# The sparse layer of a two-block model: rotation sums on GpSimd instead of VectorE, and selection rounds ahead of the last value slot

## The chip, the cores and the metric

The kernel runs on one core of one Trainium2 chip. The metric is the time of one execution on the device in microseconds; the kernel before takes 1805.46 us (median of 3 runs, 1803.48 to 1808.78). Lower is better.

PE is TensorE (the matrix engine), PEld its weight loads, DVE is VectorE, ACT is ScalarE, POOL is GpSimd, SP is SyncE, whose queue issues DMAs.

## The reference, cut to what matters

The model is a hybrid layer (window attention, a recurrent mixer, gated linear attention) followed by a block with differential attention, a feed-forward layer, a sparse attention layer and a second feed-forward layer. Only the sparse layer is touched. With 528 tokens (16 meta tokens and 512 others; padding is left out by the kernel) it computes:

```python
q, k, v, qi, ki, wi = jnp.split(h @ w_in, DSA_SPLITS, axis=-1)
q = apply_rope(q.reshape(B, T, DSA_HEADS, DSA_HEAD_DIM), cos, sin) * (DSA_HEAD_DIM ** -0.5)
k = apply_rope(k.reshape(B, T, DSA_HEADS, DSA_HEAD_DIM), cos, sin)
qi = apply_rope(qi.reshape(B, T, IDX_HEADS, IDX_DIM), cos, sin)
ki = apply_rope(rms_norm(ki, idx_k_norm), cos, sin)
...
raw = jnp.einsum('bqhd,bkd->bqhk', qib, ki).astype(f32) * (IDX_DIM ** -0.5)
score = jnp.einsum('bqhk,bqh->bqk', jax.nn.relu(raw), wb.astype(f32))
...
top_val, top_idx = lax.top_k(score, topk)          # topk = 128
# attention of each query over its 128 selected keys only

def apply_rope(x, cos, sin):
    x1, x2 = jnp.split(x.astype(jnp.float32), 2, axis=-1)
    return jnp.concatenate([x1 * c - x2 * s, x2 * c + x1 * s], axis=-1)
```

## The kernel before, in words

**Projection of the sparse layer.** PE works through 29 groups, g0 to g28, each one weight slot: g0 is the index key, g1 to g4 the index queries, g5 to g12 the queries, g13 to g20 the keys, g21 to g28 the values. Each group is 8 k steps of 6 matmuls (two column halves, three products of high and low parts; L603 to L605). Three pairs of PSUM banks are used in turn, so group g may start only when DVE has read group g-3 (`dsa_free`, semaphores `rope_read` and `v_ch`).

**Weights.** POOL issues for each group a load of the slot that was freed (`high_load`, L1004, waits for `slot_used`), ACT writes its negative (L1049), and POOL issues an accumulating load onto that (`low_sum`, L1011, waits for `w_negated`). Four slots are in flight.

**Rotations.** `rope(i, ...)` on DVE takes two groups each. i is 8 and 9 for the index queries (400 columns), 10 to 13 for the queries and 14 to 17 for the keys (528 columns). Four products read PSUM and the tables (L1358 to L1361; the last signals `rope_read`), and then the difference and the sum of products in SBUF follow (L1363, L1364; the last signals `rope_done`). On `rope_done` SP issues eight DMAs that place the heads (`dsa_scatter`, L1815, signals `scattered`). The first index score of PE, inside g7 behind its second k step, waits until both index-query scatters (8 and 9) have landed.

**Index scores and selection.** For each of four tiles of queries (n = 1, 4, 2, 3) four units of two score matmuls (L945) are placed between the k steps of g7 to g12; ACT takes the relu (L1271), DVE adds the weighted result (`index_sums`, L1665 and L1667). ACT may reuse a relu buffer only when DVE has added the unit two before. Then DVE finds the 128 best keys: 14 rounds per tile (`take_eight`: MAX8 at L1678, match and replace at L1679), and one instruction at the end of a tile makes a mask (L1682). 56 rounds in all. The table `ROUNDS_AT` says how many rounds stand behind the work of each group; those that are left stand between the value slots (`rounds_between`). DVE executes in program order.

**Behind the projection.** DVE scales each value group (L1714), PE turns it (L639) and ACT copies it (L1103, L1104). Then `dsa_attention` runs: scores on PE (L656), minimum and bias on DVE (L1502, needs the masks), exponentials on ACT (L1181), normalising on DVE (L1512), transposes on PE (L669), values on PE (L689). DVE's first L1502 stands in program order behind every selection round.

Of the kernel before, what the change touches and what calls it, by code (L numbers as in the profile page):

```python
# [18 lines left out]
T2 = T1 + META  # L19
# [43 lines left out]
S_DSA = S_DOWN0 + N_DOWN  # L63
# [6 lines left out]
def build(nc, ins, out_t):  # L70
# [3 lines left out]
    ALU = mybir.AluOpType  # L74
# [8 lines left out]
    def sem(name):  # L83
        return ctx.enter_context(nc.semaphore(name))
# [245 lines left out]
    LATER = slice(P, T2)  # L330
# [20 lines left out]
    def rope_t(i, j):  # L351
        return rope_buf[:, i % 2, j, :]
# [29 lines left out]
    S = {n: sem(n) for n in names}  # L382
# [9 lines left out]
    def halves(v):  # L392
        return v.rearrange("p (a b) -> p a b", a=2)
# [100 lines left out]
        return min((n + 1) * P, T2)  # L494

    G_QI, G_Q, G_K, G_V = 1, 5, 13, 21
    ROUNDS_AT = {8: 3, 10: 4, 12: 3, 13: 2, 14: 3, 15: 2, 16: 3, 17: 2, 18: 2, 19: 2, 20: 2}
    IDX_UNITS = [(n, p) for n in (1, 4, 2, 3) for p in range(4)]
    IDX_AT = {7: (0, 4), 8: (4, 8), 9: (8, 10), 10: (10, 12), 11: (12, 14), 12: (14, 16)}

# [60 lines left out]
    def w_turn(n):  # L561
        return (n - S_DA) % W_RING, 16 * ((n - S_DA) // W_RING + 1)

    def split_at(n):
        r = w_turn(n)[0]
        return w_hi[:, r, :], w_lo[:, r, :]
# [428 lines left out]
    def pool_block2(pool):  # L995
        g = nc.gpsimd

        def high_load(n):

            if n >= N_SLOTS:  # L1000
                return
            if n >= S_DA + W_RING:
                pool.wait_ge(S["slot_used"], n - W_RING + 1)
            g.dma_start(split_at(n)[0], ins["weights"][n]).then_inc(hi_loaded[w_turn(n)[0]], 16)  # L1004

        def low_sum(n):

            if n >= N_SLOTS:
                return
            pool.wait_ge(S["w_negated"], n - S_DA + 1)  # L1010
            g.dma_start(split_at(n)[1], ins["weights"][n], accum_op=ALU.add).then_inc(lo_summed[w_turn(n)[0]], 16)  # L1011

        def output_rests(base):

            for k in range(KT):
                pool.wait_ge(S["o_hi"], base + k + 1)
                g.tensor_tensor(o_lo[:, k, :], oT[:, k, :], o_hi[:, k, :].bitcast(F32), ALU.subtract).then_inc(S["o_split"], 1)

        pool.wait_ge(S["hn_ready"], 3 * KT)
        for n in range(S_DA, S_DA + W_RING):  # L1020
            high_load(n)
        for n in range(S_DA, S_DA + W_RING - 1):
            low_sum(n)
        pool.wait_ge(S["norm_var"], 3)
        g.memset(da_qlast, 0.0).then_inc(S["zeroed"], 1)
        for n in range(S_DA, N_SLOTS):
            if n == S_DSA + 6:
                pool.wait_ge(S["norm_var"], 5)
                g.memset(qlast, 0.0).then_inc(S["zeroed"], 1)
            if n == S_DSAO:  # L1030
                output_rests(8)
            high_load(n + W_RING)
            low_sum(n + W_RING - 1)


    def weight_high(act, n):
# [266 lines left out]
    def vector_block2(ve, st):  # L1303
        V = nc.vector
# [39 lines left out]
        def rope(i, s0, g):  # L1344

            ve.wait_ge(S["slot_used"], s0 + g + 2)
            if i >= 2:
                ve.wait_ge(scattered[i % 2], 128 * (i // 2))
            if i in (8, 9):
                a, b = (psum[:, 2 * (x % 3), 0:NL] for x in (g, g + 1))  # L1350
                c, s = cosT[:, LATER], sinT[:, LATER]
                x0, x1, x2, x3 = whole = [rope_t(i, j)[:, LATER] for j in range(4)]
            else:
                a, b = pair(g), pair(g + 1)
                c, s = cos2, sin2
                whole = [rope_t(i, j) for j in range(4)]
                x0, x1, x2, x3 = (halves(x) for x in whole)
            V.tensor_tensor(x0, a, c, ALU.mult)  # L1358
            V.tensor_tensor(x1, b, s, ALU.mult)
            V.tensor_tensor(x2, a, s, ALU.mult)  # L1360
            V.tensor_tensor(x3, b, c, ALU.mult).then_inc(S["rope_read"], 1)  # L1361
            ve.wait_ge(S["rope_read"], i + 1)
            V.tensor_tensor(whole[0], whole[0], whole[1], ALU.subtract)  # L1363
            V.tensor_tensor(whole[3], whole[3], whole[2], ALU.add).then_inc(S["rope_done"], 1)  # L1364

        def values(s0, g0, base):

# [320 lines left out]
        taken = 0  # L1688
        for g in range(7, G_V + 1):
            if g % 2:  # L1690
                i = 10 + (g - 7) // 2
                rope(i, S_DSA, g - 2)
                if i == 16:
                    ve.wait_ge(S["zeroed"], 3)
                    for c in range(2):
                        r = slice(64 * c, 64 * c + 64)
                        last = V.tensor_copy(qlast[r, :, 16 * c:16 * c + 16], qs[r, :, 4 * P:T2])
                    last.then_inc(S["q_last"], 1)
            for u in range(*IDX_AT.get(g, (0, 0))):
                index_sums(u)  # L1700
            for r in range(taken, taken + ROUNDS_AT.get(g, 0)):
                take_eight(r)
            taken += ROUNDS_AT.get(g, 0)
        left = 4 * ROUNDS - taken

        def rounds_between(j):

            for r in range(taken + left * j // 8, taken + left * (j + 1) // 8):
                take_eight(r)
        for j in range(8):  # L1710
            ve.wait_ge(S["slot_used"], S_DSA + G_V + j + 1)
            if j >= 2:
                ve.wait_ge(S["v_tr"], 8 + j - 1)
            V.tensor_tensor(halves(vch[:, j % 2, :]), pair(G_V + j), rs2, ALU.mult).then_inc(S["v_ch"], 1)  # L1714
            rounds_between(j)
        dsa_attention()
        residual(5, S_DSAO, 1, 16, lambda k: col("ffn_norm", 8 + k))
        ffn(1, 5, S_UP1, S_DOWN1, 24)
# [1308 lines left out]
```

## Time and profile before

| | |
|---|---|
| median of 3 runs | 1805.46 us |
| the profiled execution | 1798.56 us |
| its span, first to last instruction | 1796.8 us |
| mean granted clock of TensorE | 0.975 |
| PE busy | 1713.8 us (95%) |
| DVE busy | 949.0 us (53%) |
| ACT busy | 632.5 us (35%) |
| POOL busy | 330.8 us (18%) |

The span is what the trace covers; the profiled execution has 1.8 us around it. Busy times of a span say which engine is full on average. For a change in one stage what counts is which engine ends last there, and that is read from gaps in PE's timeline and from what ended them.

### The profile page before, as it was taken

Reading aid. Unit: us, or ns where it says so; the run is one execution under the profiler, and the core shown is the slowest. Engines: PE = TensorE matmul, PEld = TensorE weight load, DVE = VectorE, ACT = ScalarE, POOL = GpSimd, SP = SyncE. Lnnn points to the kernel's source line nnn. Section 1 sums busy time; section 2 is a strip of 40 time slices with the busy share of each in tenths; the row PEclk is TensorE's granted clock in tenths of the full one; section 3 lists DMA queues with packets and bytes.
Section 4 is the critical chain, followed back from the end, with each engine's and each line's share of the span. In section 5 each row is a group of like instructions: output and inputs, shape, how many; then the busy total and the mean of one; then the engine's idle time right before and its main releaser. Section 6 shows DMA issues by size and latency. Waiting matters only on the chain.

```text
span 1796.8 us, 33090 instructions
## 1 busy us (share of the span) xinstructions
PE 1713.8 (95%) x14293; PEld 1537.7 (86%) x14293; DVE 949.0 (53%) x1881; ACT 632.5 (35%) x1095; POOL 330.8 (18%) x450
## 2 busy tenths in 40 slices
PE   7999989979998899999999999999899999999997
PEld 3777679859996589999999998799669999999886
DVE  5237695435335865655562115787883555565003
ACT  3354442243114653222222222322584322222222
POOL 0001102001220012222222222122012222222221
PEclk9999969899998999999999999999999999999999
DMA  7521400126994039898888999699305888898995
GB/s 301 177 76 59 176 1 4 61 53 145 226 207 93 1 69 195 181 180 184 180 184 185 199 194 203 145 212 210 79 2 111 175 184 186 181 185 182 197 209 139
DMA packets 81794, 266.46 MB, mean 148 GB/s; under 512 B 11648, under 2 KB 15360, under 8 KB 81520
## 3 DMA queue, kind: packets, MB, share of 16 engines
q0 software_dynamic: 59040, 214.98, 56.7%
q1 hardware_dynamic: 18592, 43.57, 7.0%
q10 hardware_dynamic: 4016, 5.78, 1.1%
q8 instruction: 113, 1.85, 0.4%
q14 instruction: 33, 0.27, 0.0%
HBM read 252.49 MB, written 2.10 MB: 142 GB/s over the span
## 4 chain that ended last, share of the span: by engine, by line
PE 76%; DVE 7%; issue 2%; DMA 1%; ACT 1%; POOL 0%; ACTq 0%; DVEq 0%; POOLq 0%
PE banks L603 21%; PE banks L604 20%; PE banks L605 20%; PE banks L2090 3%; PE banks L656 1%; PE banks L669 1%; DMA w_lo<-in_weights 1%; DVE stat L1407 1%; PE banks L689 1%; PE banks L1845 1%; PE banks L1847 1%; PE banks L1846 1%; PE banks L732 1%; PE banks L945 1%; DVE arena L1417 1%
## 5 line engine op out<-in xcount | busy, mean ns | idle before, releaser
L603 PE MATMUL banks<-hn_hi,w_hi 128*128 128x264 f32 (+2 forms) x2216 | 637.9, 288 | 14.4 <-DMA w_lo<-in_weights 12.8
L604 PE MATMUL banks<-hn_lo,w_hi 128*128 128x264 f32 (+2 forms) x2216 | 631.4, 285 | 0.0
L605 PE MATMUL banks<-hn_hi,w_lo 128*128 128x264 f32 (+2 forms) x2216 | 630.8, 285 | 0.0
L1049 ACT ACTIVATE w_lo<-w_hi 128x1024 fp32r<-128x1024 f32 x205 | 217.2, 1060 | 771.9 <-DMA w_hi<-in_weights 757.3
L603 PEld LDWEIGHTS banks<-hn_hi,w_hi 128*128 128x128 f32 x2216 | 419.0, 189 | 26.8 <-issue 22.3
L604 PEld LDWEIGHTS banks<-hn_lo,w_hi 128*128 128x128 f32 x2216 | 420.2, 190 | 0.7 <-issue 0.2
L605 PEld LDWEIGHTS banks<-hn_hi,w_lo 128*128 128x128 f32 x2216 | 417.9, 189 | 0.3
L1004 POOL DMA_DIRECT2D w_hi<-in_weights x205 | 114.1, 557 | 915.3 <-PE banks L605 840.3
L1011 POOL DMA_DIRECT2D w_lo<-in_weights x205 | 180.8, 882 | 156.1 <-ACT w_lo L1049 146.8
L603 PE MATMUL banks<-a_hi,w_hi 128*128 128x264 f32 (+1 forms) x506 | 160.4, 317 | 1.6 <-DVE u_in L1576 0.8
L604 PE MATMUL banks<-a_lo,w_hi 128*128 128x264 f32 (+1 forms) x506 | 160.8, 318 | 0.0
L605 PE MATMUL banks<-a_hi,w_lo 128*128 128x264 f32 (+1 forms) x506 | 160.7, 318 | 0.0
L603 PEld LDWEIGHTS banks<-a_hi,w_hi 128*128 128x128 f32 x506 | 95.3, 188 | 8.5 <-DVE u_in L1576 1.0
L605 PEld LDWEIGHTS banks<-a_hi,w_lo 128*128 128x128 f32 x506 | 95.2, 188 | 6.6
L604 PEld LDWEIGHTS banks<-a_lo,w_hi 128*128 128x128 f32 x506 | 95.0, 188 | 6.8
L1301 DVE TENSOR_TENSOR ring_r<-ring,ring_r 128x1024 fp32r<-128x1024 f32 x32 | 39.6, 1236 | 80.5 <-ACT ring_r L1043 80.4
L1578 DVE TENSOR_TENSOR u_in<-banks,rs 128x516 f32<-128x516 f32 x44 | 30.6, 695 | 90.5 <-PE banks L605 90.4
L1576 DVE TENSOR_TENSOR u_in<-banks,rs 128x528 f32<-128x528 f32 x44 | 31.1, 707 | 88.5 <-PE banks L605 88.4
L1846 PE MATMUL banks<-h_r,ring_r 128*128 128x512 f32 x192 | 76.0, 396 | 0.0
L603 PE MATMUL banks<-o_hi,w_hi 128*128 128x264 f32 (+1 forms) x256 | 73.3, 286 | 1.4 <-DMA w_lo<-in_weights 0.8
L604 PE MATMUL banks<-o_lo,w_hi 128*128 128x264 f32 (+1 forms) x256 | 72.6, 284 | 0.0
L605 PE MATMUL banks<-o_hi,w_lo 128*128 128x264 f32 (+1 forms) x256 | 72.4, 283 | 0.0
(426 smaller groups left out, 2702.5 us busy)
## 6 DMA issues: line engine op xcount, KB each, us to landing
w_hi<-in_weights POOLq DMA_DIRECT2D x205, 512.0 KB, 5.2
w_lo<-in_weights POOLq DMA_DIRECT2D x205, 512.0 KB, 7.2
ring<-in_weights SPq DMA_DIRECT2D x49, 512.0 KB, 4.5
arena<-arena ACTq DMA_DIRECT2D x64, 66.0 KB, 5.3
arena<-arena SPq DMA_DIRECT2D x64, 66.0 KB, 4.9
arena<-in_gate_w SPq DMA_DIRECT2D x8, 512.0 KB, 3.5
h<-in_xT SPq DMA_DIRECT2D x2, 1024.0 KB, 6.3
arena<-in_alibi SPq DMA_DIRECT2D x1, 1024.0 KB, 7.7
```

Of the source, the lines that this page charges most:

```text
L603: mm(o, w[0][:, j, :], x[0][:, k, lo:hi], start=first, stop=False)
L604: mm(o, w[0][:, j, :], x[1][:, k, lo:hi], start=False, stop=False)
L605: ins_ = mm(o, w[1][:, j, :], x[0][:, k, lo:hi], start=False, stop=last)
L656: last = mm(psum[:, 2 * (v % 2) + c, 0:keys(n)], qs[r, p, n * P:(n + 1) * P], kz[r, p, 0:keys(n)], start=True, stop=True)
L1004: g.dma_start(split_at(n)[0], ins["weights"][n]).then_inc(hi_loaded[w_turn(n)[0]], 16)
L1011: g.dma_start(split_at(n)[1], ins["weights"][n], accum_op=ALU.add).then_inc(lo_summed[w_turn(n)[0]], 16)
L1049: nc.scalar.activation(split_at(n)[1], split_at(n)[0].bitcast(F32), ACT.Copy, scale=-1.0).then_inc(S["w_negated"], 1)
L1301: nc.vector.tensor_tensor(ring_lo(n), ring_slot(n), ring_hi(n).bitcast(F32), ALU.subtract).then_inc(S["w_split_d"], 1)
L1576: V.tensor_tensor(halves(u_in[:, g % 4, 2:T2 + 2]), pair(g), rs2, ALU.mult).then_inc(S["u_evac"], 1)
L1578: V.tensor_tensor(halves(u_in[:, g % 4, KEEP + 2:T2 + 2]), kept_pair(g), halves(rs[:, KEEP:T2]), ALU.mult).then_inc(S["u_evac"], 1)
L1846: mm(out, w[0][:, k, :], x_lo, start=False, stop=False)
L2090: last = mm(out(s), lhs[r], rhs[r], start=start, stop=stop)
```

## The change

Ten rotations of the sparse layer (i = 8 to 17) lose their last two instructions on DVE. POOL executes them in a new function `rope_sums`, placed behind the `high_load` and the `low_sum` of iterations 3, 5, ..., 21 of the sparse layer's groups: iteration 3 for i = 8, iteration 5 for i = 9, and so on. SP's scatters still wait for `rope_done`, which POOL now signals.

The table of rounds changes, and the rounds that are left (28 before, 20 now) are spread over seven value slots instead of eight, so that none stands behind the last.

```diff
-    ROUNDS_AT = {8: 3, 10: 4, 12: 3, 13: 2, 14: 3, 15: 2, 16: 3, 17: 2, 18: 2, 19: 2, 20: 2}
+    ROUNDS_AT = {8: 4, 10: 5, 12: 5, 13: 2, 14: 4, 15: 2, 16: 3, 17: 2, 18: 4, 19: 2, 20: 3}
+    SUMS_AT = tuple(range(3, 23, 2))
...
+        def rope_sums(i):
+
+            t = LATER if i < 10 else slice(0, T2)
+            x0, x1, x2, x3 = (rope_t(i, j)[:, t] for j in range(4))
+            pool.wait_ge(S["rope_read"], i + 1)
+            g.tensor_tensor(x0, x0, x1, ALU.subtract)
+            g.tensor_tensor(x3, x3, x2, ALU.add).then_inc(S["rope_done"], 1)
...
             high_load(n + W_RING)
             low_sum(n + W_RING - 1)
+            if n - S_DSA in SUMS_AT:
+                rope_sums(SUMS_AT.index(n - S_DSA) + 8)
...
             V.tensor_tensor(x3, b, c, ALU.mult).then_inc(S["rope_read"], 1)
+            if i >= 8:
+                return
             ve.wait_ge(S["rope_read"], i + 1)
-            V.tensor_tensor(whole[0], whole[0], whole[1], ALU.subtract)
-            V.tensor_tensor(whole[3], whole[3], whole[2], ALU.add).then_inc(S["rope_done"], 1)
+            V.tensor_tensor(rope_t(i, 0), rope_t(i, 0), rope_t(i, 1), ALU.subtract)
+            V.tensor_tensor(rope_t(i, 3), rope_t(i, 3), rope_t(i, 2), ALU.add).then_inc(S["rope_done"], 1)
...
-            for r in range(taken + left * j // 8, taken + left * (j + 1) // 8):
+            for r in range(taken + left * j // 7, taken + left * (j + 1) // 7):
                 take_eight(r)
...
-            rounds_between(j)
+            if j < 7:
+                rounds_between(j)
```

**POOL, around the sums of rotation 9.** These are POOL's instructions behind g4 and g5, before; w_hi is the load of a slot, w_lo the accumulating one, and the memset prepares a buffer of the attention.

```order
L1004 DMA w_hi<-in_weights 128x1024 [waits slot_used]
L1011 DMA w_lo<-in_weights 128x1024 [waits w_negated]
L1004 DMA w_hi<-in_weights 128x1024 [waits slot_used]
L1011 DMA w_lo<-in_weights 128x1024 [waits w_negated]
L1029 MEMSET arena 128x256 [waits norm_var]
```

The same place now:

```order
L1005 DMA w_hi<-in_weights 128x1024 [waits slot_used]
L1012 DMA w_lo<-in_weights 128x1024 [waits w_negated]
L1005 DMA w_hi<-in_weights 128x1024 [waits slot_used]
L1012 DMA w_lo<-in_weights 128x1024 [waits w_negated]
L1025 TENSOR_TENSOR arena<-arena 128x400 [waits rope_read]
L1026 TENSOR_TENSOR arena<-arena 128x400
L1038 MEMSET arena 128x256 [waits norm_var]
```

The sums of rotation 9 stand behind a load that waits for the end of g5, on an engine that had no such work there.

**DVE, between the index sums in g12 and rotation 13.** Before, three rounds of the first tile stand there, then the four products and the two sums:

```order
L1671 TENSOR_TENSOR arena<-arena,causalf 128x128 [waits i_acc]
L1672 MEMSET arena 128x16
L1678 MAX top<-arena 128x8 [waits dve_step]
L1679 MATCH_REPLACE arena<-top,arena 128x240 [waits dve_step]
L1678 MAX top<-arena 128x8 [waits dve_step]
L1679 MATCH_REPLACE arena<-top,arena 128x240 [waits dve_step]
L1678 MAX top<-arena 128x8 [waits dve_step]
L1679 MATCH_REPLACE arena<-top,arena 128x240 [waits dve_step]
L1358 TENSOR_TENSOR arena<-banks,arena 128x528 [waits scattered1,slot_used,dve_step]
```

Now there are five, with the mask instruction of the tile behind them (of the five, the last three):

```order
L1690 MAX top<-arena 128x8 [waits dve_step]
L1691 MATCH_REPLACE arena<-top,arena 128x240 [waits dve_step]
L1690 MAX top<-arena 128x8 [waits dve_step]
L1691 MATCH_REPLACE arena<-top,arena 128x240 [waits dve_step]
L1690 MAX top<-arena 128x8 [waits dve_step]
L1691 MATCH_REPLACE arena<-top,arena 128x240 [waits dve_step]
L1694 TENSOR_SCALAR arena<-arena 128x256 [waits dve_step]
L1368 TENSOR_TENSOR arena<-banks,arena 128x528 [waits scattered1,slot_used,dve_step]
L1369 TENSOR_TENSOR arena<-banks,arena 128x528
L1370 TENSOR_TENSOR arena<-banks,arena 128x528
L1371 TENSOR_TENSOR arena<-banks,arena 128x528
```

Two rounds and the mask instruction moved ahead of the first product of rotation 13.

**DVE, behind the last value slot.** Before, four rounds (here the last two) and the mask stand between the scaling of the last slot and the first score unit of the attention:

```order
L1678 MAX top<-arena 128x8 [waits dve_step]
L1679 MATCH_REPLACE arena<-top,arena 128x496 [waits dve_step]
L1678 MAX top<-arena 128x8 [waits dve_step]
L1679 MATCH_REPLACE arena<-top,arena 128x496 [waits dve_step]
L1682 TENSOR_SCALAR arena<-arena 128x512 [waits dve_step]
L1502 ISA arena,stat<-banks,causalf 128x128 [waits a_sc,sel_spread,dve_step]
```

Now:

```order
L1690 MAX top<-arena 128x8 [waits dve_step]
L1691 MATCH_REPLACE arena<-top,arena 128x496 [waits dve_step]
L1694 TENSOR_SCALAR arena<-arena 128x512 [waits dve_step]
L1726 TENSOR_TENSOR arena<-banks,rs 128x528 [waits v_tr,slot_used,dve_step]
L1514 ISA arena,stat<-banks,causalf 128x128 [waits a_sc,sel_spread]
```

The last scaling stands directly ahead of the attention's first instruction.

## Rows read from the trace of the kernel before

**Rows 1.** Windows: length, busy PE, PEld, DVE, ACT, POOL, clock, DMA, GB/s.

```profile
1123.00:1181.00 58.00, 56.50 (x389) 44.34 (x388) 41.97 (x91) 21.16 (x39) 10.35 (x15) 1.00 0.68 155
1181.00:1228.00 47.00, 46.66 (x386) 46.69 (x387) 41.31 (x85) 8.32 (x8) 11.37 (x16) 1.00 0.99 224
```

**Rows 2.** Timeline, PE: start, us, line, tile, count, [idle before and its releaser].

```profile
1124.22 0.68 PE L945 MATMUL banks<-arena 64*128 64x240 f32 x4 [1.11 <-issue]
1181.35 0.36 PE L603 MATMUL banks<-hn_hi,w_hi 128*128 128x264 f32 x1 [0.71 <-DVE arena L1361]
...
1274.03 0.93 PE L656 MATMUL banks<-arena 64*128 64x128 f32 x8
1279.56 3.36 PE L656 MATMUL banks<-arena 64*128 64x384 f32 x8 [4.60 <-DVE stat L1502]
```

**Rows 3.** Timeline, DVE, from the last value slot to the attention.

```profile
1271.98 0.71 DVE L1714 TENSOR_TENSOR arena<-banks,rs 128x528 f32<-128x528 f32 x1 [1.12 <-issue]
...
1278.53 0.43 DVE L1682 TENSOR_SCALAR arena<-arena 128x512 f32<-128x512 f32 x1
1278.99 0.29 DVE L1502 CUSTOM_DVE_ANT_0 arena<-banks,causalf 128x128 f32<-128x128 f32 x1
...
1282.22 0.16 DVE L1509 RECIPROCAL stat<-stat 128x2 f32<-128x2 f32 x1
```

**Rows 4.** Timeline, ACT, the first exponentials of the attention.

```profile
1274.89 1.28 ACT L1181 ACT_TABLE_LOAD   x1
1279.33 0.40 ACT L1181 ACTIVATE arena<-arena,stat 128x128 f32<-128x128 f32 x1 [3.15 <-DVE stat L1502]
```

**Rows 5.** Timeline, SP: the first and last of rotation 9's eight scatters.

```profile
1113.30 0.51 SPq L1815 DMA_DIRECT2D arena<-arena  x1
1117.66 0.59 SPq L1815 DMA_DIRECT2D arena<-arena  x1
```

**Rows 6.** Line L1815: landing of all 80, then of the one at 1117.66.

```profile
DMA to landing us min/median/max: 2.0/4.7/7.3
DMA to landing us min/median/max: 6.5/6.5/6.5
```

**Rows 7.** Timeline, POOL, behind g5.

```profile
1116.17 0.55 POOL L1004 DMA_DIRECT2D w_hi<-in_weights  x1 [4.36 <-PE banks L605]
1116.71 0.91 POOL L1011 DMA_DIRECT2D w_lo<-in_weights  x1
1117.25 0.69 POOL L1029 MEMSET arena<- 128x256 f32 x1
```

**Rows 8.** Lines by shape, POOL: busy us, mean ns; idle before.

```profile
L1017 POOL TENSOR_TENSOR o_lo<-arena,o_hi 128x528 fp32r<-128x528 f32 x8 | 10.4, 1310 | 77.3 <-ACT o_hi L1199 77.3
L2254 POOL TENSOR_TENSOR arena<-norm_tmp 128x256 f32<-128x256 f32 x7 | 6.4, 910 | 0.0
```

**Rows 9.** Windows behind two gaps of PE: clock is the third from last.

```profile
429.00:433.00 4.00, 3.99 (x20) 3.99 (x21) 1.17 (x4) 1.06 (x1) 0.87 (x1) 0.57 1.06 236
1279.50:1282.80 3.30, 3.24 (x8) 1.19 (x8) 2.20 (x12) 2.63 (x11) 0.00 (x0) 0.50 0.00 0
```

**Rows 10.** Timeline, PE, the gap ahead of the first of these windows.

```profile
429.01 0.39 PE L603 MATMUL banks<-hn_hi,w_hi 128*128 128x264 f32 x1 [2.39 <-DMA w_lo<-in_weights]
```

**Rows 11.** Timeline, DVE: index sums, rounds, products of rotation 11.

```profile
1142.88 1.51 DVE L1667 SCALAR_TENSOR_TENSOR arena<-arena,wtok 16x512 f32<-16x512 f32 x2 [1.11 <-ACT arena L1271]
...
1144.64 0.41 DVE L1678 MAX8 top<-arena 128x8 f32<-128x240 f32 x1
...
1147.50 0.71 DVE L1358 TENSOR_TENSOR arena<-banks,arena 128x528 f32<-128x528 f32 x1
...
1149.35 0.69 DVE L1361 TENSOR_TENSOR arena<-banks,arena 128x528 f32<-128x528 f32 x1
...
1157.27 1.24 DVE L1667 SCALAR_TENSOR_TENSOR arena<-arena,wtok 128x368 f32<-128x368 f32 x2 [2.28 <-ACT arena L1271]
...
1173.91 1.50 DVE L1667 SCALAR_TENSOR_TENSOR arena<-arena,wtok 128x496 f32<-128x496 f32 x2 [2.63 <-ACT arena L1271]
```

More of the change, by code:

```diff
@@ L1351, in rope @@
                 c, s = cosT[:, LATER], sinT[:, LATER]
-                x0, x1, x2, x3 = whole = [rope_t(i, j)[:, LATER] for j in range(4)]
+                x0, x1, x2, x3 = (rope_t(i, j)[:, LATER] for j in range(4))
             else:
@@ L1355, in rope @@
                 c, s = cos2, sin2
-                whole = [rope_t(i, j) for j in range(4)]
-                x0, x1, x2, x3 = (halves(x) for x in whole)
+                x0, x1, x2, x3 = (halves(rope_t(i, j)) for j in range(4))
             V.tensor_tensor(x0, a, c, ALU.mult)
```

## The prediction

> **What bounds the kernel now.** I read the window view first, then the gaps in PE's timeline, then what stands around each gap on the other engines. In the projection of the sparse layer PE is the engine that ends last: from 1123 to 1181 us it is busy 56.5 of 58 us at the full clock while DVE has 42 and POOL 10 [rows 1]. So work taken off DVE is worth nothing there by itself. What counts are the few gaps of PE, and there are four that the change touches [rows 2]: 1.11 us ahead of the first index score in g7, no gap but little margin at g10, 0.71 us at the start of g14 behind the products of rotation 13, and 4.60 us ahead of the attention's third score unit, which waits for DVE. Each is priced below. One more thing is to be seen in the windows: behind a gap of some us PE may run at the lower of its two levels, 1.2 instead of 2.4 GHz.
>
> Times are those of the profiled execution, which lasts 1798.56 us with a span of 1796.8; the median of the runs is 6.9 us above. I work out a difference and add it to the median.
>
> **Part 1, no rounds behind the last value slot.** DVE scales the last value group at 1271.98, ends four rounds at 1278.53 (some 1.48 us each) and a mask of 0.43, and starts the first score unit at 1278.99 [rows 3]. PE has the first two score units done in the 0.93 us from 1274.03 [rows 2], so the first of them is there at about 1274.5, and DVE could start at 1274.6: 4.4 us earlier. Who is late next? ACT: its table load is a row from 1274.89 for 1.28 us, so its first exponential can start at 1276.2 and not before, against 1279.33 now [rows 4]: 3.1 us earlier. But PE gains as well. Its third and fourth score units took 3.36 us at the lower level [rows 2, 9], because a gap of 4.60 stood ahead of them; with a gap of about half a microsecond I take them at full clock, 1.7 us. DVE's third unit then ends near 1277.0, the first exponentials near 1277.1, and normalising starts at 1277.1 where it started at 1282.22 [rows 3]: 5.1 earlier. ACT, 3.1 earlier at first, has the table load behind it after that and only follows DVE; I take it that it makes up the rest within the first units. So -5.0 us. Bounds: -3.1 if ACT stays the late one, and -6.1 if the 4.4 and the whole 1.7 of clock came through. The rounds that moved ahead between the value slots cost nothing: three rounds and the scaling are 5.2 us, and a value group is longer on PE, as the 1.12 us of idle ahead of the last scaling, behind three rounds of this size, shows [rows 3].
>
> **Part 2, the sums of rotation 9 and the first index score.** Now SP's scatters of rotation 9 are issued from 1113.30, the last at 1117.66 [rows 5]; that last one lands 6.5 us after its issue [rows 6], at 1124.1, and PE's first index score starts at 1124.22 after waiting 1.11 [rows 2]. The trace calls the releaser "issue"; the two times agree to 0.1 us, so I take it for this landing. In the changed order the sums stand on POOL behind the load that waits for the end of g5 (1116.17) and the accumulating load (1116.71). The memset that stands at that place starts at 1117.25 [rows 7], and so can the sums. No row shows a sum of 400 columns on POOL: 528 columns take 1.31 us, 256 take 0.91 [rows 8], so between 0.91 and 1.31, and by interpolation 1.1; two end at 1119.4. That is 6.1 us later than SP's start now. The eight issues take 4.4 to the last (1113.30 to 1117.66), so the last is issued at 1123.8. Its landing is the unknown: all 80 lie between 2.0 and 7.3 us [rows 6]. A scatter issued right behind a pair of weight loads was the slow one (6.5, with the pair at 1116.17 and 1116.71), and the next pair is issued within half a microsecond of 1123.8, so I take 5.4. The landing is at 1129.2, with bounds 1125.8 and 1131.1; PE starts again at 1129.3 where it started at 1124.22. That is +5.1 us, bounds +1.7 and +7.0. PE cannot use the wait, since its instructions are executed in order and the scores stand in front of the rest of g7. What it costs beyond the wait is the clock. The gap is 6.2 us. Behind a gap of 2.39 the window of 4 us ran at a mean of 0.57, which is about 3.4 us at half level [rows 9, 10], and behind 4.60 there were 3.3 us at 0.50 [rows 9]. Behind 1.11 and 0.71 nothing was lost. Half of 3.4 is +1.7 us; bounds 0 and +2.1. Part 2 together: +6.8.
>
> Rotation 8's sums wait on POOL for their products, which DVE finishes late, so that scatter moves by 1 us only and stays ahead of rotation 9's. The other eight scatters also start later, but what waits for them is the rotation two further, four groups away. POOL's weight loads move by nothing: a pair of sums of 528 columns is 2.6 us and POOL idles 4.36 us ahead of such a load [rows 7].
>
> **Part 3, more rounds where DVE has no room.** In g7 to g12 DVE's index sums are tied to PE through ACT: the idle of 1.11, 2.28 and 2.63 us ahead of them [rows 11] is where the 1.3 us that each rotation saves on DVE vanish. Behind the last index sum of a group nothing is saved, and what is added there is late in full. A round of the first tile costs 0.95 us (three from 1144.64 to 1147.50). At g8 one is added: the last product of rotation 11 ends at 1150.04 now [rows 11] and would end 0.95 later, against PE's own course. PE shows no gap at g10 now, so it gets there at 1150.1 or later, and how much later no row tells: between 0 and +0.95, and I take the middle, +0.5. At g10 one is added ahead of rotation 12's products; PE shows no gap at g12, and DVE idles 2.28 inside g10 [rows 11]: 0 (to +0.95). At g12 two are added and the tile's mask, 0.3 us (one of 512 columns takes 0.43 [rows 3]): 2 x 0.95 + 0.3 = 2.2. PE already waits 0.71 for exactly these products at g14 [rows 2], so all of it is on the path: +2.2 (1.9 to 2.4), and the gap becomes 2.9. Between g13 and g15 six rounds of 1.5 us and the four products of 2.5 give 11.4, against two groups of PE. A group has 48 matmuls, and a window of 47 us without scores holds 386 of them [rows 1], 5.84 a group, 11.7 for two: no wait, though with little to spare. From there on DVE does no more between two rotations than that.
>
> **A rule that speaks against the change.** The idle that covers DVE's index sums is between 1.11 and 2.63 us [rows 11], and the sums of rotations 10 to 12 on POOL would lie beside them. The Trainium skill (GPSIMD Engine Reference, Key points) states that GpSimd shares its SBUF interfaces with VectorE and that the two contend where a DVE instruction has two SBUF inputs, as the index sums have. No row of before shows the two side by side in this stage. By that rule a rotation could hold DVE for up to POOL's 2.6 us, of which 2.28 is covered at rotation 11: 0.3 us more in the sum, which I leave out.
>
> **The sum.** -5.0 + 5.1 + 1.7 + 0.5 + 2.2 = +4.5 us: 1805.46 + 4.5 = 1810.0. A difference of 0.3% or 5.4 us is about what a measurement of this kernel can tell from none, so this is "within 0.3%", on the slow side.
>
> **Rivals.**
> 1. Two clock drops: slower by over 0.3%. The gap at g14 grows to 2.9 us, and a gap of 2.39 was enough once [rows 9, 10]. If the level falls there too, another 1.7 is paid. It decides from a gap of somewhere between 1.11 and 2.39. Against it: that gap stood in another stage, with the DMA queues late. With it +4.5 + 1.7 = +6.2, and with the landing at its late bound +8.1: about 1812.6. Chance 0.43, including a landing near the late bound without the second drop.
> 2. The landing is early: the last scatter lands in 2.0 us and the level stays. Part 2 is +1.7, the sum -5.0 + 1.7 + 0.5 + 2.2 = -0.6: 1804.9. For it speaks the low end of the 80 landings, against it the weight loads issued at the same time. Chance 0.12, within 0.3%.
> 3. What ended PE's wait at 1124.1 was not the landing, so the later sums cost nothing: -5.0 - 0.4 + 0 to 2.2, some -3 to -6: about 1801. For it: the releaser is not named. Against: the agreement to 0.1 us, and that the code has PE wait for this. Chance 0.07, which I count as faster.
> 4. The forecast itself: 0.38.
>
> Faster by over 0.3%: 0.07; within: 0.50 (the forecast and rival 2); slower: 0.43. The sum of all low bounds is 1.7 + 0 + 0 + 1.9 - 6.1 = -2.5, of all high bounds 7.0 + 2.1 + 0.95 + 0.95 + 2.4 + 1.7 - 3.1 = +12. Both ends at once are unlikely; I give -1 to +10.5, that is 1804.5 to 1816.
>
> **What would show it.** PE's gap ahead of the first index score: 6 us instead of 1.1, with SP's scatters of rotation 9 issued from about 1119.4, and the clock at half for some 3 us behind it. The gap at g14: 2.9 instead of 0.7, released by the fourth product of rotation 13. A gap of under 0.5 us at g10. The gap of 4.60 ahead of the attention's third unit gone, and the full clock there. The eight 528-column sums of POOL near 1.3 us. The prediction is wrong if the gap in g7 stays near 1 us, if the attention starts less than 3 us earlier against the end of g28, or if DVE's index sums grow beside POOL's.

## The result and the profile after

The changed kernel takes 1808.7 us (median of 17 runs, 1803.5 to 1814.9), beside 1801.4 us for the kernel before (17 runs, 1794.0 to 1808.8). The ratio is 1.0044, with a 95% interval of 1.0031 to 1.0057: by it the change is 7.9 us slower (5.6 to 10.3); the two medians by themselves are 7.3 us apart. The forecast was +4.5, 1810.0 us; the sign and the mechanism were right, and rival 1, with a second clock drop, is nearer in size.

One execution of each has a trace. The one of before took 1798.56 us, the one of the change 1804.37, a difference of 5.8; but the part ahead of the stage was 2.8 us shorter in the second. So I measure the stage between two marks on PE, one ahead of and one behind everything that was changed: the fold matmul ahead of the index queries' end, and the first group of four transposes in the attention. PE's timeline, before and then the change:

```profile
1103.43 1.13 PE L929 MATMUL banks<-arena,fold 128*128 128x512 f32 x2 [0.91 <-DVE arena L1646]
...
1285.06 0.66 PE L669 MATMUL banks<-ident,arena 128*128 128x128 f32 x4 [1.25 <-DVE arena L1512]
```

```profile
1100.59 0.70 PE L930 MATMUL banks<-arena,fold 128*128 128x512 f32 x1 [1.55 <-DVE arena L1658]
...
1127.62 1.17 PE L946 MATMUL banks<-arena 64*128 64x240 f32 x4 [7.37 <-issue]
...
1156.63 0.36 PE L604 MATMUL banks<-hn_hi,w_hi 128*128 128x264 f32 x1 [0.97 <-DVE arena L1371]
...
1190.05 0.36 PE L604 MATMUL banks<-hn_hi,w_hi 128*128 128x264 f32 x1 [2.96 <-DVE arena L1371]
...
1285.49 1.82 PE L657 MATMUL banks<-arena 64*128 64x384 f32 x8 [0.29 <-DVE stat L1514]
...
1290.09 0.66 PE L670 MATMUL banks<-ident,arena 128*128 128x128 f32 x4 [1.09 <-DVE arena L1524]
```

The stage took 1285.06 - 1103.43 = 181.6 us and now takes 1290.09 - 1100.59 = 189.5: 7.9 us longer, the same as by the ratio. Three of the gaps of [rows 2] are there again, larger or smaller (1.11, 0.71 and 4.60 are now 7.37, 2.96 and 0.29), and there is one at g10 that had been none. Between the marks the 7.9 divide so:

| stretch | before | after | more | of it |
|---|---|---|---|---|
| fold to first index score | 20.79 | 27.03 | +6.2 | gap 1.11 to 7.37 |
| to the start of g14 | 57.13 | 62.43 | +5.3 | g10 0.97, g14 2.25, the rest (2.1) clock |
| to DVE's last scaling | 90.63 | 92.18 | +1.6 | clock |
| to the first normalising | 10.24 | 5.18 | -5.1 | no rounds, clock at full |
| to the second mark | 2.84 | 2.68 | -0.2 | |

The clock is the third number from the last in these windows of the change; they stand inside g7's gap, behind it, behind the gap at g14, and at the attention's start:

```profile
1124.00:1127.60 3.60, 0.00 (x0) 0.01 (x1) 0.00 (x0) 0.00 (x0) 0.00 (x0) 0.71 0.88 184
1127.60:1132.20 4.60, 4.58 (x18) 3.73 (x20) 0.81 (x2) 0.63 (x2) 0.00 (x0) 0.50 0.02 4
1190.00:1194.00 4.00, 3.96 (x20) 3.99 (x21) 3.83 (x9) 1.06 (x1) 2.57 (x2) 0.57 0.97 226
1284.00:1290.00 6.00, 3.88 (x26) 1.68 (x23) 4.67 (x23) 5.59 (x17) 0.00 (x0) 1.00 0.72 168
```

Behind the first gap 4.6 us ran at 1.2 GHz, behind the second 4.0 us at a mean of 0.57. That is 2.3 and 1.7 us of PE's time, close to the 2.1 and 1.6 left over in the table. The attention, which ran at 0.50 before [rows 9], runs at 1.00. In the last 3.6 us of PE's wait in g7 every engine stands: DVE, ACT and POOL have 0.00.

Why it stands is read on POOL and SP. POOL behind g5, in the change (answers to [rows 7]):

```profile
1113.32 0.55 POOL L1005 DMA_DIRECT2D w_hi<-in_weights  x1 [4.31 <-PE banks L606]
...
1114.42 1.42 POOL L1025 TENSOR_TENSOR arena<-arena 128x400 f32<-128x400 f32 x1
1115.43 1.41 POOL L1026 TENSOR_TENSOR arena<-arena 128x400 f32<-128x400 f32 x1
```

SP's first and last scatter of rotation 9, and, from the view of that line, the landing of the last:

```profile
1116.87 0.51 SPq L1828 DMA_DIRECT2D arena<-arena  x1
...
1121.22 0.59 SPq L1828 DMA_DIRECT2D arena<-arena  x1
```

```profile
DMA to landing us min/median/max: 6.3/6.3/6.3
```

The sums stand behind the load that waits for PE's end of g5, and end at 1116.84. SP issues from 1116.87, the last at 1121.22; it lands 6.3 us later, at 1127.5, and PE starts at 1127.62. Counted from the fold, SP starts at 16.3 instead of 9.9, 6.4 later.

DVE at the end of the projection, answering to [rows 3], and ACT, answering to [rows 4]:

```profile
1282.23 0.71 DVE L1726 TENSOR_TENSOR arena<-banks,rs 128x528 f32<-128x528 f32 x1 [0.86 <-PE banks L606]
...
1284.92 0.29 DVE L1514 CUSTOM_DVE_ANT_0 arena<-banks,causalf 128x128 f32<-128x128 f32 x1 [1.99 <-PE banks L657]
...
1287.41 0.16 DVE L1521 RECIPROCAL stat<-stat 128x2 f32<-128x2 f32 x1
```

```profile
1285.14 1.28 ACT L1192 ACT_TABLE_LOAD   x1
1286.44 0.40 ACT L1192 ACTIVATE arena<-arena,stat 128x128 f32<-128x128 f32 x1
```

The rows between scaling and score units are gone; DVE now waits 1.99 us for PE.

What I had left out of the sum is on DVE beside POOL's sums. These are the index sums behind rotation 11's products, first before and then in the change; the last two index sums behind rotation 12's; and the mask of a later tile beside the sums of a later rotation. Behind them stand POOL's sums of rotation 11:

```profile
1151.84 3.15 DVE L1667 SCALAR_TENSOR_TENSOR arena<-arena,wtok 128x368 f32<-128x368 f32 x5
```

```profile
1156.84 6.12 DVE L1679 SCALAR_TENSOR_TENSOR arena<-arena,wtok 128x368 f32<-128x368 f32 x5
1163.69 1.24 DVE L1679 SCALAR_TENSOR_TENSOR arena<-arena,wtok 128x368 f32<-128x368 f32 x2 [0.74 <-ACT arena L1282]
...
1180.37 1.51 DVE L1679 SCALAR_TENSOR_TENSOR arena<-arena,wtok 128x496 f32<-128x496 f32 x2 [0.17 <-ACT arena L1282]
...
1216.26 3.55 DVE L1694 TENSOR_SCALAR arena<-arena 16x528 f32<-16x528 f32 x1
```

```profile
1157.06 1.67 POOL L1025 TENSOR_TENSOR arena<-arena 128x528 f32<-128x528 f32 x1
1158.36 1.64 POOL L1026 TENSOR_TENSOR arena<-arena 128x528 f32<-128x528 f32 x1
```

Five index sums take 6.12 us where they took 3.15: the 3.0 us lost on DVE are the length of POOL's pair, 2.94 us from 1157.06 to 1160.00. The idle that covered DVE's index sums, 2.28 at this place [rows 11], is down to 0.74, and one group later 2.63 is down to 0.17. It is not used up, so PE does not see it; but at rotation 12 little is left.

Each of these POOL sums is recorded with 1.6 to 1.7 us where 1.31 was known [rows 8]. That is not DVE's doing. The two sums of 400 columns above took 1.42 and 1.41 while DVE stood idle (it has no instruction between 1109.3 and 1118.85). In the change the long ones are those directly behind a load that POOL has just issued; those of rotations 8 and 13, for which POOL waited on DVE first, took 1.05 and 1.31. In both cases the second sum starts as soon behind the first (1.01 and 1.3 us); it is the end of the last one that comes some 0.4 us later. Why was not tried.

### The profile page after: what moved, and what is told of

Same layout as the page of the kernel before. It is cut to its first block, busy times and chain, and to the rows that moved or that the text cites. A ratio compares the mean times of both kernels' runs of the same rounds, so it can differ in the third digit from the quotient of the medians.

```text
span 1802.5 us, 33090 instructions
## 1 busy us (share of the span) xinstructions
PE 1714.8 (95%) x14293; PEld 1540.8 (85%) x14293; DVE 948.9 (53%) x1861; ACT 632.5 (35%) x1095; POOL 356.2 (20%) x470
## 4 chain that ended last, share of the span: by engine, by line
PE 76%; DVE 7%; issue 2%; DMA 1%; ACT 1%; POOL 0%; ACTq 0%; DVEq 0%
PE banks L604 20%; PE banks L605 20%; PE banks L606 20%; PE banks L2103 3%; DMA w_lo<-in_weights 1%; PE banks L670 1%; PE banks L657 1%; DVE stat L1419 1%; PE banks L690 1%; PE banks L1858 1%; PE banks L1859 1%; PE banks L1860 1%; PE banks L946 1%; PE banks L733 1%; DVE arena L1429 1%
```

## The experiments

My theory: the wait in g7 and the clock behind it are the loss, and they come from where the sums of rotations 8 and 9 stand on POOL, not from how long they take. The rivals: contention between POOL and DVE makes DVE late; or the rounds in their new places do. Each ratio is against the kernel before, run beside it; "us" is that ratio times the median of the kernel before. "Stage" is the time between the two marks in the one trace, against 181.6 before.

| | ratio (95%) | us | stage |
|---|---|---|---|
| the change | 1.0044 (1.0031 to 1.0057) | +7.9 | +7.9 |
| e1 rounds only | 0.9996 (0.9976 to 1.0017) | -0.7 | -0.1 |
| e2 sums only | 1.0022 (1.0006 to 1.0038) | +4.0 | +8.6 |
| e3 change, 8 and 9 back on DVE | 0.9970 (0.9953 to 0.9987) | -5.4 | -0.9 |
| e4 change, 9 one place earlier | 0.9987 (0.9970 to 1.0004) | -2.3 | +4.6 |
| e5 before, with idle sums on POOL | 1.0027 (1.0010 to 1.0044) | +4.9 | +5.9 |
| e6 rounds fitted, sums on DVE | 0.9952 (0.9939 to 0.9966) | -8.7 | -6.7 |
| e7 the same, 13 to 17 on POOL | 0.9961 (0.9941 to 0.9980) | -7.0 | -5.5 |
| e8 only 8 and 9 on POOL | 1.0043 (1.0026 to 1.0060) | +7.8 | +8.8 |
| e9 change with fitted rounds | 1.0001 (0.9983 to 1.0019) | +0.2 | +2.8 |
| e10 e6 with two queues | 0.9963 (0.9940 to 0.9985) | -6.7 | -5.8 |

The stage column is on average 2.3 us above the other. One trace of before is behind all of it, so its stage may simply have been a short one; a term of under 2 us is therefore read from gaps and not from a median. Some of it is the clock: the traces of e4, e8, e9 and e10 lost 1.7 to 3.4 us at the very start of the stage, where the edits change nothing or next to nothing, and the one of before did not. The column also leaves out what comes behind the second mark. There the traces of e1, e6 and e10 fell to 1.2 GHz, at a cost of 1.7 us each; this is e1:

```profile
1286.00:1289.00 3.00, 3.00 (x16) 1.76 (x14) 2.22 (x9) 1.61 (x8) 0.00 (x0) 0.50 0.00 0
```

The traces of the change, e3, e4, e7 and e9 have the same short gaps of PE ahead of that place (0.84 and 1.09 us) and lost nothing. So the full clock in the attention is not a sure part of what the end gives back.

**e1 and e2: the two halves.** e1 is the kernel before with the new table and seven slots; e2 is the change with the old ones.

```diff
-    ROUNDS_AT = {8: 3, 10: 4, 12: 3, 13: 2, 14: 3, 15: 2, 16: 3, 17: 2, 18: 2, 19: 2, 20: 2}
+    ROUNDS_AT = {8: 4, 10: 5, 12: 5, 13: 2, 14: 4, 15: 2, 16: 3, 17: 2, 18: 4, 19: 2, 20: 3}
...
-            for r in range(taken + left * j // 8, taken + left * (j + 1) // 8):
+            for r in range(taken + left * j // 7, taken + left * (j + 1) // 7):
                 take_eight(r)
...
-            rounds_between(j)
+            if j < 7:
+                rounds_between(j)
```

> The table of rounds and the seven slots of the change, with all sums back on VectorE. Theory (the waits of TensorE price the change): no long gap ahead of the first index score (1.1 us as before), the attention starts 5.0 us earlier against the last value slot; g10 waits 0.9, g14 waits 2.9 with one clock drop (1.7), and g16 waits about 1.0, since six rounds, two sums and four products are 12.7 us against 11.7 of TensorE. Sum -5.0 + 0.9 + 2.2 + 1.7 + 1.0 = +0.8 us against before. Rival (GpSimd and VectorE contend for the SBUF interface, and that is what the change costs): without GpSimd's sums the 5 us of the end come through, -5 us.

PE's timeline of e1:

```profile
1124.69 0.68 PE L945 MATMUL banks<-arena 64*128 64x240 f32 x4 [1.46 <-issue]
...
1151.60 0.36 PE L603 MATMUL banks<-hn_hi,w_hi 128*128 128x264 f32 x1 [0.96 <-DVE arena L1361]
...
1185.00 0.36 PE L603 MATMUL banks<-hn_hi,w_hi 128*128 128x264 f32 x1 [2.95 <-DVE arena L1361]
...
1197.77 0.36 PE L603 MATMUL banks<-hn_hi,w_hi 128*128 128x264 f32 x1 [0.92 <-DVE arena L1361]
```

The gaps at g10 and g14 are those of the change to 0.01 us, with no sum on POOL: they belong to the rounds alone. At g16 there is one of 0.92 that the change does not have; there the saved sums are what hides a round. The three gaps cost about what the end gives back, and 0.9996 says the same, within some 4 us either way. One thing differs: behind this gap of 2.95 us no clock was lost.

```profile
1185.00:1189.00 4.00, 4.00 (x33) 4.00 (x34) 3.90 (x8) 1.06 (x1) 0.00 (x0) 1.00 1.02 242
```

The same edit the other way round, in the change (e2):

```diff
-    ROUNDS_AT = {8: 4, 10: 5, 12: 5, 13: 2, 14: 4, 15: 2, 16: 3, 17: 2, 18: 4, 19: 2, 20: 3}
+    ROUNDS_AT = {8: 3, 10: 4, 12: 3, 13: 2, 14: 3, 15: 2, 16: 3, 17: 2, 18: 2, 19: 2, 20: 2}
```

> The ten pairs of sums on GpSimd as in the change, with the old table and the old eight slots. Theory: the gap ahead of the first index score is 7.4 us as in the change, with the clock at half behind it; g14 waits 0.7 as before, g10 nothing; the gap of 4.6 us ahead of the attention's third unit stays. Sum +6.3 + 1.7 = +8.0 us against before. Rival (contention): VectorE's index sums grow by 3 us per rotation and what they delay makes up part of it: gaps at g10 or g14 larger than before.

PE's timeline of e2:

```profile
1131.03 1.17 PE L946 MATMUL banks<-arena 64*128 64x240 f32 x4 [7.38 <-issue]
...
1288.66 1.65 PE L657 MATMUL banks<-arena 64*128 64x384 f32 x4 [4.60 <-DVE stat L1514]
```

The wait in g7 is there in full, and the others are as before (0.72 at g14, 4.60 in the attention). Its trace has +8.6, its median only +4.0 (1.1 to 6.9): slower, but by less than expected, and that stays open.

**e8: rotations 8 and 9 alone on POOL**, the old rounds, all else on DVE. In the change:

```diff
-    SUMS_AT = tuple(range(3, 23, 2))
+    SUMS_AT = (3, 5)
...
-            g.tensor_tensor(x3, x3, x2, ALU.add).then_inc(S["rope_done"], 1)
+            g.tensor_tensor(x3, x3, x2, ALU.add).then_inc(S["pool_done"], 1)
...
-            if i >= 8:
+            if i in (8, 9):
                 return
```

(SP waits for `pool_done` for these two, and the table and the slots are those of before.)

> Only the sums of rotations 8 and 9 on GpSimd, at the places of the change; those of 10 to 17 on VectorE, old table, old eight slots. Theory (the change's cost is the first index score): the gap ahead of it is 7.4 us, with one clock drop, the others as before: +6.3 + 1.7 = +8 us. Rival (the run with all ten on GpSimd measured only +4, so the drop or part of the wait is often absent): +4 us, with a shorter gap. If contention had been in that run's time, this one is faster than it.

PE's timeline, and the window behind the gap:

```profile
1131.06 1.17 PE L946 MATMUL banks<-arena 64*128 64x240 f32 x4 [6.16 <-issue]
```

```profile
1131.00:1136.50 5.50, 5.44 (x22) 4.04 (x23) 0.81 (x2) 0.81 (x3) 0.00 (x0) 0.51 0.50 121
```

1.0043: these four instructions, moved from DVE to POOL, make by themselves a loss as large as the whole change. Without the other eight rotations on POOL it is not faster than e2, so contention is not what e2 pays for. The gap is 1.2 us shorter than in e2, because the last scatter landed 5.1 us behind its issue and not 6.3. Of the 8.8 in the trace 1.7 is not the edit's: behind a gap of 1.25 us ahead of the first mark this window ran at a mean of 0.72 (0.28 of 6.0).

```profile
1104.00:1110.00 6.00, 5.81 (x25) 5.21 (x25) 2.56 (x9) 1.06 (x1) 2.27 (x3) 0.72 0.83 189
```

**e3: those two back on DVE**, with their two instructions each behind the products again, and the change otherwise:

```diff
-    SUMS_AT = tuple(range(3, 23, 2))
+    SUMS_AT = tuple(range(7, 23, 2))
...
-            if i >= 8:
+            if i >= 10:
                 return
```

> The change with the sums of rotations 8 and 9 back on VectorE; GpSimd keeps those of 10 to 17. Theory: the gap ahead of the first index score is 1.1 us again, the rest as in the change: -5.0 + 1.0 + 2.25 + 1.7 = -0.1 us against before, some 8 us faster than the change. Rival (contention): the index sums still grow by 3 us beside GpSimd, and the kernel stays clearly slower than before, +4 us or more.

PE's timeline of e3, then DVE's, and the window behind the gap at g14:

```profile
1123.48 0.68 PE L946 MATMUL banks<-arena 64*128 64x240 f32 x4 [1.77 <-issue]
...
1150.39 0.36 PE L604 MATMUL banks<-hn_hi,w_hi 128*128 128x264 f32 x1 [0.96 <-DVE arena L1371]
...
1183.78 0.36 PE L604 MATMUL banks<-hn_hi,w_hi 128*128 128x264 f32 x1 [2.96 <-DVE arena L1371]
```

```profile
1150.60 6.12 DVE L1681 SCALAR_TENSOR_TENSOR arena<-arena,wtok 128x368 f32<-128x368 f32 x5
```

```profile
1183.80:1187.80 4.00, 4.00 (x33) 4.00 (x34) 3.83 (x9) 1.06 (x1) 2.53 (x2) 1.00 0.96 210
```

The long wait is gone, and what remains is faster than before (0.9970). The index sums still take 6.12 us and the gap at g10 is still the 0.96 of e1, which has no sum on POOL: contention is real and costs nothing here. The gap of 2.96 again lost no clock. I had expected -0.1, with a second clock drop of 1.7 in it that this trace does not have. The median is 4.5 us below what the trace's stage gives; beyond the 2.3 that holds for the column, this is open.

**e4: the sums of rotation 9 one place earlier**, behind the loads that wait for g4:

```diff
-    SUMS_AT = tuple(range(3, 23, 2))
+    SUMS_AT = (3, 4) + tuple(range(7, 23, 2))
```

> The change with GpSimd's sums of rotation 9 one iteration ahead, behind the loads that follow g4 instead of g5. Theory (the place in GpSimd's queue sets the wait): the sums start when their products are there, SP starts about 1.2 us later than before the change instead of 6.4, and the gap ahead of the first index score is 2 to 3 us instead of 7.4; one clock drop may go with it. Sum -5.0 + 1.5 + 1.0 + 2.25 + 1.7 = +1.5, with a drop in g7 +3.2 us against before. Rival (GpSimd's slower arithmetic or its DMA work makes the sums late wherever they stand): the gap stays above 5 us.

POOL's timeline at the sums of rotation 9, and PE's at the first index score:

```profile
1115.81 1.05 POOL L1025 TENSOR_TENSOR arena<-arena 128x400 f32<-128x400 f32 x1 [0.40 <-DVE arena L1371]
1116.82 1.05 POOL L1026 TENSOR_TENSOR arena<-arena 128x400 f32<-128x400 f32 x1
```

```profile
1128.61 1.17 PE L946 MATMUL banks<-arena 64*128 64x240 f32 x4 [1.95 <-issue]
```

On POOL the sums now wait for DVE's product and not for a load, and PE's gap is 1.95 us, not 7.37. The sums are still there, recorded 0.4 us shorter each now that POOL idles just ahead of them: it is their place in POOL's queue that cost. Its trace lost clock from 1104 on (3.4 us of PE's time), behind the 1.95 us in g7 (1.7) and behind a gap of 2.95 at g14 (1.7; a mean of 0.57 over 4 us). The median has less of it: by the ratios e4 is 10.2 us faster than the change (-2.3 against +7.9).

**e5: contention by itself.** The kernel before, with eight pairs of two-input operations of 528 columns on POOL where the change has the sums of rotations 10 to 17. They work on an unused tile and nothing reads what they write.

```diff
+            if n - S_DSA in range(7, 23, 2):
+                ...
+                for a in range(2):
+                    g.tensor_tensor(sq[:, a, :], sq[:, 0, :], sq[:, 1, :], ALU.subtract).then_inc(S["idle_sum"], 1)
```

> The kernel before, and on GpSimd eight extra pairs of 528-column two-input operations on a buffer nobody uses, at the places where the change has the sums of rotations 10 to 17; VectorE keeps all its work and all rounds stand where they did. It prices the contention alone. Theory (contention is real and hidden): VectorE's five index additions of 368 columns take 6.1 us instead of 3.15, those of 496 columns 7.2 instead of 3.8, the gaps of TensorE stay 1.1, 0.7 and 4.6 us but for some tenths at g14, and the time is that of before within 0.1% (-1 to +2 us). Rival (contention costs time): +4 us or more, with new gaps at g10 to g16. If the additions keep their length, there is no contention.

PE's timeline, and DVE's at rotation 13:

```profile
1182.86 0.36 PE L603 MATMUL banks<-hn_hi,w_hi 128*128 128x264 f32 x1 [1.18 <-DVE arena L1369]
...
1234.51 0.36 PE L603 MATMUL banks<-hn_hi,w_hi 128*128 128x264 f32 x1 [1.48 <-DVE arena L1369]
```

```profile
1182.75 2.61 DVE L1371 TENSOR_TENSOR arena<-arena 128x528 f32<-128x528 f32 x1
1185.28 1.83 DVE L1372 TENSOR_TENSOR arena<-arena 128x528 f32<-128x528 f32 x1
```

My expectation fell. PE waits at five rotations (0.47 more, 0.63, 1.29, 0.87, 1.48, together 4.7 us), and the median is +4.9. DVE's own sums of 0.7 us each took 2.61 and 1.83 beside POOL's. So two inputs from SBUF on both engines cost PE time as soon as DVE is near its limit. In the change they do not, because there DVE has given its sums away and has products from PSUM and rounds at these places, which keep their length (one mask does not, at 1216.26 above, and PE shows no gap behind it). The Trainium skill (GPSIMD Engine Reference, Key points) states that the two engines contend where DVE's instruction has two SBUF inputs; the rows agree, and the page gives no size for it.

**e6: rounds placed without POOL.** Since e1's gaps are products that come too late, I counted rounds to DVE's room at each place and left the sums on DVE:

```diff
-    ROUNDS_AT = {8: 3, 10: 4, 12: 3, 13: 2, 14: 3, 15: 2, 16: 3, 17: 2, 18: 2, 19: 2, 20: 2}
+    ROUNDS_AT = {8: 3, 10: 4, 12: 2, 13: 3, 14: 3, 15: 2, 16: 3, 17: 2, 18: 3, 19: 2, 20: 3}
...
-            for r in range(taken + left * j // 8, taken + left * (j + 1) // 8):
+            first = taken + sum((4, 4, 4, 4, 4, 3, 3)[:j])
+            for r in range(first, first + (4, 4, 4, 4, 4, 3, 3)[j]):
                 take_eight(r)
...
-            rounds_between(j)
+            if j < 7:
+                rounds_between(j)
```

> All sums on VectorE, none of the change's GpSimd work; rounds placed by room: 3 at g8, 4 at g10, 2 at g12, then 3, 3, 2, 3, 2, 3, 2, 3, and 4, 4, 4, 4, 4, 3, 3 between the value slots, none behind the last. Theory: the gap at g14 (0.7) goes, no gap at g10 and g16, the attention starts 5.0 us earlier: -5.7 us or 0.9968 of before. Rival (VectorE has no room for the rounds without GpSimd's help): new gaps of more than 1 us in the key groups or the value slots, and less than 3 us gained.

PE's timeline, and two windows:

```profile
1121.70 0.68 PE L945 MATMUL banks<-arena 64*128 64x240 f32 x4 [0.67 <-issue]
...
1271.72 1.82 PE L656 MATMUL banks<-arena 64*128 64x384 f32 x8 [0.29 <-DVE stat L1502]
```

```profile
1116.00:1180.00 64.00, 63.32 (x448) 51.26 (x447) 44.81 (x95) 22.24 (x40) 11.73 (x16) 1.00 0.71 159
1180.00:1268.00 88.00, 88.00 (x733) 87.89 (x733) 80.65 (x175) 20.16 (x27) 20.01 (x28) 1.00 0.96 212
```

0.9952 (0.9939 to 0.9966), faster than both kernels: the end's 5 us are taken, and from 1180 on PE is busy 88.00 of 88 us, with no gap at g10, g14 or g16. Nothing had to go to POOL for it. I had expected -5.7; of the -6.7 in the trace 5.1 is the end, 0.7 the gap at g14 and 0.4 the smaller gap in g7. The -8.7 by the median is more than these give, and that is open.

**e7 and e9: what POOL adds to that.** e7 is e6 with the sums of rotations 13 to 17 on POOL, e9 is the change (all ten on POOL) with e6's rounds.

```diff
-    SUMS_AT = tuple(range(3, 23, 2))
+    SUMS_AT = tuple(range(13, 23, 2))
```

> The same rounds as the run with all sums on VectorE, and the sums of rotations 13 to 17 on GpSimd, behind the index scores. Theory: VectorE is not the bound there, so 1.24 us less per rotation changes nothing: -5.7 us, equal to that run within 0.1%. Rival (GpSimd's sums do help): 1 us or more faster than that run; a third way (contention on the rounds and masks): slower than it by 1 us or more.

0.9961 (0.9941 to 0.9980): not to be told from e6. Where PE does not wait for DVE, DVE's saved 1.3 us a rotation are worth nothing.

> The change with all ten pairs of sums on GpSimd, and the rounds placed by room as in the fitted runs (3 at g8, 4 at g10, 2 at g12). Theory: the wait ahead of the first index score stays (7.4 us, clock drop behind it), the waits at g10 and g14 go, the attention starts 5.0 us earlier: +6.3 + 1.7 - 0.7 - 5.0 = +2.3 us against before. Against the change itself that is 3.9 us for the two waits and 1.7 for the second drop, where it happens. Rival (the wait at g14 was only hidden slack that the first wait creates): +6 us or more.

PE's timeline of e9, and the window behind the gap:

```profile
1131.21 1.17 PE L946 MATMUL banks<-arena 64*128 64x240 f32 x4 [6.54 <-issue]
```

```profile
1131.00:1137.00 6.00, 5.79 (x26) 4.51 (x27) 0.99 (x3) 1.27 (x4) 0.00 (x0) 0.58 0.06 12
```

The wait in g7 and 2.5 us of clock (0.42 of 6.0) come back and eat the gain: 1.0001 (0.9983 to 1.0019).

**e10: the last gap.** e6 with four of rotation 9's eight scatters issued from ACT's queue:

```diff
+            if g == 4:
+                act.wait_ge(S["rope_done"], 10)
+                for r in range(4):
+                    ...
+                    act.dma_start(qi_sb[at:at + 32, (4 + r) // 2, LATER], src[32 * r:32 * r + 32, LATER]).then_inc(scattered[1], 16)
...
+                    if i == 9 and half:
+                        continue
```

> The fitted kernel with all sums on VectorE, and four of the eight scatters of rotation 9 issued from ScalarE's queue while SyncE's issues the other four. Theory (the last issue sets the first index score): the last is issued at 2.5 us behind the sum instead of 4.4, ahead of the next pair of weight loads, so it lands before TensorE asks and the gap of about 1 us goes: 1.1 us faster than the fitted kernel, -7.9 against before by my sums, or 0.9946 where that one measured 0.9952. Rival (the landing follows the weight loads, not the issue): no difference.

The gap ahead of the first index score is gone, but 0.9963 (0.9940 to 0.9985) is no better than e6's ratio, where 1.1 us more had been expected. A term of about 1 us is below what these runs can tell.

## Why the prediction was right, and where its sizes were off

The measured ratio lies outside the 0.3% that I had given the better chance (0.50), and in the class that I had given 0.43, slower by more. What made the difference is in points 3, 5 and 7.

1. **What bounds.** Right. PE ends last, and the loss is where it had gaps. e7 shows that DVE's saved time is worth nothing.
2. **End of the projection, -5.0.** Measured -5.1, from the last scaling to the first normalising, by the steps forecast: ACT's table load follows its last copy at once (1285.14), the clock stays at 1.00, the gap of 4.60 is 0.29. The clock in it was partly luck: e1 and e6 had the same early start and fell to 1.2 GHz some 3 us later.
3. **The wait in g7, +5.1.** The mechanism is shown four times: alone in e8 (+7.8), removed in e3 (-5.4), shortened by a place in POOL's queue in e4 (gap 1.95), brought back in e9. The size is 6.2. Of the 1.1 missing, 0.3 is the start of SP's scatters (6.4 later, not 6.1: the pair of sums took 2.4 us, directly behind a load's issue and with DVE idle, and not 2.2), the rest is the landing, 6.3 us where I took 5.4. Between 2.0 and 7.3 I had gone to a value below the row that this scatter resembles, the one of 6.5 with weight loads just ahead, and that row was the better guess.
4. **Its clock, +1.7.** Measured 2.1 by the marks, 2.3 by the window; at the upper bound given.
5. **g10, +0.5.** Measured 0.97, the upper bound, where "a gap of under 0.5 us" had been given as a sign: PE had no margin there at all. e1 and e3 show the same gap.
6. **g14, +2.2.** Measured 2.25, the gap 2.96 and not 2.9.
7. **No second drop.** This is the step that failed: I gave it as rival 1, and in the change's trace it was there (1.6 to 1.7). But of four traces with a gap of 2.95 to 2.96 at g14, two lost clock (the change, e4) and two did not (e1, e3). The two that lost it had lost it in g7 too, some 62 us earlier, and the two that did not had not. Whether that is the cause was not tried.
8. **g16, none "with little to spare".** Right in the change. e1, without the saved sums, has 0.92 there.
9. **Contention, left out.** Right in the sum, for the reason given: the idle ahead of the index sums shrank from 2.28 to 0.74 and from 2.63 to 0.17. But the growth of DVE's index sums was one of the signs by which I would have been wrong, and they did grow, by 3.0 us, more than the 2.6 that I had set as the limit. What I had not seen is that cover is all that made it harmless. e5 shows that it is no small matter where DVE has sums of its own.

6.2 + 2.1 + 1.0 + 2.25 + 1.6 - 5.1 - 0.2 = +7.9, against 4.5: 1.1 from the gap, 0.4 from its clock, 0.5 from g10 and 1.6 from the second drop, less 0.2.

Open: why e2's and e3's medians lie 4.5 us below their traces' stages, and e4's 6.9, and what decides over the clock behind a gap of 3 us.

## What to carry to other kernels

An operation given to an idle engine takes over the waits of that engine's queue: before moving it, read what stands ahead of it there, and count from the release of that to whoever needs the result. Here four short instructions, set behind a load that waits for PE, cost PE 6 us and its clock. And where the aim is room at one end, look first whether the work can be spread to fit the room that there is; that gave 8.7 us (6.1 to 11.0) with nothing moved between engines.

## What the runs showed of the hardware that was not expected

- **The size of the contention.** Beside a pair of POOL sums of 528 columns, index sums on DVE (two SBUF inputs) took 6.12 us for five instead of 3.15. A mask, which reads one tensor in SBUF, took 3.55 us in the change, where the largest one alone takes 0.43 [rows 3]. The selection's instructions and the products from PSUM kept their 0.7 us. What DVE lost each time was about the time from the start of POOL's pair to its end, 2.9 us. POOL's own sums show no such loss: their longer records, 1.42 for 400 columns and 1.6 to 1.7 for 528, come with DVE idle (1114.42) or at its rounds (1.65 at 1228.79) too, and follow a load that POOL has just issued.
- **What the low clock costs depends on where it begins.** Behind gaps of 6 to 7 us PE ran at 1.2 GHz for 4.6 us in the change and for some 5.3 us in e8. But the granted clock had fallen while PE still stood, and the whole stretch at 0.50 was 6.8 us in both, about 1125.5 to 1132.3 and 1129.5 to 1136.3. What lies inside the wait is free; the rest costs PE half its length.
- **Short gaps can cost the clock too.** Behind the 1.25 us ahead of the first mark e8 ran at a mean of 0.72 for 6 us; behind the 1.26 us at the same place e1 lost nothing. Between them the traces have a loss behind 0.98 us (e10) and none behind 1.62 (e7). The prediction's point from which a drop would decide, between 1.11 and 2.39 us, was no bound: a gap of the same length does both.
